# One head pair's gate panels as a unit of seven half-size products

## The chip, the cores and the metric

The kernel runs on one core of a Trainium2 chip. The metric is the device time of one execution in microseconds; the kernel before takes 957.01 us (median of three runs, 956.84 to 957.34).

## What is computed

One sub-layer of a streaming encoder for 512 tokens of width 1024, all in float32:

```python
h = rms_norm(x, norm_g)
proj = h @ w_in            # 1024 x 14,928, split into q, k, v, z, gates of three branches
y_a = mLSTM(...)  * sigmoid(o_a) * silu(z_a)
y_b = dsa_attention(q_b, k_b, v_b, top-k keys of an indexer) * silu(z_b)      # 8 heads of 128
y_m = memory_attention(q_m, k_m, v_m) * silu(z_m)
g   = sigmoid(gate)        # 3 x 1024 columns of proj
out = x + (g[0] * (y_a @ w_branch[0]) + g[1] * (y_b @ w_branch[1]) + g[2] * (y_m @ w_branch[2])) @ w_out
```

The change is in branch B: for each head the kernel needs 128 columns each of q, k, v and z, and beside them it computes 256 of the gate columns.

## The kernel before, in words

Every float32 matrix is used as the sum of a high and a low part (`split`: ScalarE copies the raw tile to a rounded high part, VectorE subtracts that from the raw tile to get the low part). A product is three matmuls per 128 rows of the contraction: high x high, high x low, low x high. The contraction of 1024 is cut into two halves `kh` of KH = 4 blocks. hT_hi and hT_lo hold the normalised input, features on partitions, tokens along the row.

Branch B handles its eight heads in four pairs, i = 0 to 3 (`PAIRS`). For a pair, heads r = 2i and l = 2i + 1:

- **The unit** (`b_unit`, `b_product`, L1185): q, k and v of both heads by seven half-size products instead of eight, after Strassen and Winograd. The raw weights are four blocks a, b, c, d of 4 x 384 columns (a and b: first half of the contraction, c and d: second half). GpSimd makes four sums of them in place (`b_weight_sum`, L3169, four instructions of 384 columns each). Products have tokens as the stationary and weights as the moving operand, 2 x 12 matmuls of 384 columns, into the PSUM banks `main` (0, 1) and `other` (2, 3). Between products ScalarE copies banks out (`b_save`) and VectorE adds banks to saved parts (`b_add`).
- **The two panels** (`f_panel`, L825): z of one head and 256 gate columns, with weights as the stationary and all 512 tokens as the moving operand: 3 blocks x 2 halves x 12 matmuls of 512 columns, for each of the two heads. ScalarE takes the banks out with SiLU (`z_evac`) and sigmoid (`gate_evac`).
- **Attention of the heads**, as hooks between products: `b_turn_qk` (8 transposes, L1138; waits for `b_rotated`), `b_score` (12 matmuls, L1149; waits for the split q and k), `b_turn_p` (10 transposes, L1157; waits for `b_scaled`), `b_values` (12 matmuls, L1167). Head r is done inside its own pair's panels, head l ("tail") inside the next pair's unit.

Each operand, raw, sum or panel, takes one of three slots (`b_op`), is made high on ScalarE (`b_high(n)`, L1760) and low on VectorE (`b_low(n)`, L2584), and TensorE waits for `op_low >= n + 1`. A slot is free when the product three earlier is done (`b_used`). Before the change a pair has 11 operands, `B_OPS`: 7 of the unit and 4 of the panels.

The order on each engine is written out by hand: `b_body(i)` on ScalarE and on VectorE, a list of sums, squares and powers on GpSimd, loads and stores on SyncE. Each engine takes its list strictly in order. On VectorE `b_rotary(a)` is a sum of squares (L2627), four products with the rotary tables (L2636), two joins (L2398, L2399) and the scaling of the keys (L2642, which sets `b_rotated`); it needs GpSimd's squares (L3200) and power (L3205). `b_maxes` (L2598) finds row maxima of the scores, `b_exps` (L1779, ScalarE) the exponentials, `b_scale_p` (L2606, L2609) sets `b_scaled`. The last pair, i = 3, has two small z panels instead of two wide ones, and then the branch panels follow (`branch_panel`), whose left operand y is loaded back from memory (`merged<-ym_kept`) after pair 3's stores: on SyncE the store of y for the head l of pair 2 stands ahead of that load.

Of the kernel before, what the change touches and what calls it, by code (L numbers as in the profile page):

```python
# [14 lines left out]
P = 128  # L15
S = 512
D = 1024
# [30 lines left out]
A_OPHIGH = A_OPLOW = B_OPS * PAIRS - 2  # L48
A_UDONE, A_TDONE, A_USAVED, A_UADDED, A_UREAD = 14 * PAIRS, 4 * PAIRS, 6 * PAIRS, 6 * PAIRS, 2 * PAIRS
# [65 lines left out]
BF = _plan.take(0, 0, (7, 7, 6, 0))  # L115
# [41 lines left out]
def hybrid_block(nc, x, mem, positions, norm_g, mem_norm_g, w_in, conv_w, conv_b, mlstm_gate_b,  # L157
# [3 lines left out]
    with ctx:  # L161
# [132 lines left out]
        raw_e = w_flat[0][:, :, 1536:2048]  # L294
        raw_f = w_hi_f32[:, :].rearrange("p (h n) -> p h n", h=2)[:, :, 1536:2048]
# [148 lines left out]
        def b_op(op, n):  # L444

            width = D if n >= (PAIRS - 1) * B_OPS + 7 else 1536
            return op[B_SLOT[n % 3]][:, 0:width]

        def b_raw_of(n):

            width = D if n >= (PAIRS - 1) * B_OPS + 7 else 1536
            return b_w[B_RAW[n % B_OPS]][:, 0:width]
# [19 lines left out]
        def b_used(n):  # L472

            i, m = n // B_OPS, n % B_OPS
            if m < PRODUCTS:
                return u_done, 2 * PRODUCTS * i + 2 * m + 2
            j, kh = (m - PRODUCTS) // 2, (m - PRODUCTS) % 2
            if kh == 0:
                return f_half, HALF0 + 2 * i + j + 1
            b = 1 if i == PAIRS - 1 else 2  # L480
            return proj_done[b], BF[2][b] + 2 * i + j + 1
# [33 lines left out]
        def _(sp):  # L515
# [102 lines left out]
            def f_gate_stores(i, j):  # L618
                for b in (1, 2):
                    sp.wait_ge(bank_empty[b], BF[2][b] + 2 * i + j + 1)  # L620
                    gate_store(4 + 2 * (2 * i + j) + b - 1, b - 1)
# [17 lines left out]
            for b in range(4):  # L639
                sp.wait_ge(bank_empty[b], BS[2][b] + 1)  # L640
                gate_store(b, b % 2)
            for i in range(PAIRS):
                n = B_OPS * i
# [24 lines left out]
            n = B_OPS * (PAIRS - 1)  # L668
# [7 lines left out]
            sp.wait_ge(f_half, HALF0 + 2 * PAIRS - 1)  # L676
# [135 lines left out]
        def _(pe):  # L812
# [364 lines left out]
            def b_product(i, m, lhs, to, start, before):  # L1177
                n = B_OPS * i + m
# [10 lines left out]
            def b_unit(i):  # L1189
                main, other = (banks[0], banks[1]), (banks[2], banks[3])  # L1190
                tail = 2 * i - 1
                if i:
                    b_turn_qk(tail)
                b_product(i, 0, h_block(0, 0), main, True,
                          lambda t: (bank_empty[t], BF[2][t] + 2 * i) if i else (bank_empty[t], BS[2][t] + 1))
                if i:
                    b_score(tail)
                b_product(i, 1, h_block(KH, 0), other, True,
                          lambda t: ((bank_empty[2], BF[2][2] + 2 * i), (u_added, 6 * i))[t] if i else (bank_empty[2 + t], BS[2][2 + t] + 1))
                if i == 0:  # L1200
                    pe.wait_ge(s_low, 3)
                b_product(i, 2, h_sum(0), main, False, lambda t: (u_saved, 6 * i + t + 1))
                if i:
# [2114 lines left out]
```

## Time and profile before

| | us |
|---|---|
| median of three runs | 957.01 |
| the profiled execution's own time | 957.17 |
| its span (first to last instruction) | 955.4 |
| TensorE busy in it | 950.4 |
| VectorE / ScalarE / GpSimd busy | 735.9 / 544.7 / 351.4 |

Times inside the execution count from the start of the span. A pair takes some 73 us of it; pair 2, the "third pair", has its unit from 375.11 to 409.31 us, its panels to 447.91, and pair 3's unit runs from 448.70 to 482.89. "Busy" of TensorE counts a matmul from its start to its modelled end, and matmuls overlap, so the spacing of starts is what a product costs: a count over the length of a window.

### The profile page before, as it was taken

The numbers are of one execution on the slowest core, as the hardware profiler recorded it, in microseconds if no ns is written. First come the engines' busy times: TensorE is split into PE (matmuls) and PEld (weight loads), VectorE is DVE, ScalarE is ACT, GpSimd is POOL, SyncE is SP. The second block draws the span as 40 slices with busy tenths as digits, with TensorE's granted clock in tenths as the row PEclk, the third lists the DMA queues.
The fourth block names the chain that finished last, engine by engine and source line by source line (L and its number), as shares of the span: only waits on it lengthen the run. The fifth ranks groups of instructions, "written<-read, shape, count | busy, mean of one in ns | idle before, by whom it ended". The sixth has DMA issues, their size and how long they took to land.

```text
span 955.4 us, 13764 instructions
## 1 busy us (share of the span) xinstructions
PE 950.4 (99%) x5041; PEld 843.6 (88%) x5041; DVE 735.9 (77%) x1110; ACT 544.7 (57%) x834; POOL 351.4 (37%) x246
## 2 busy tenths in 40 slices
PE   9999999999999999999999999999999999999998
PEld 7888888888989988988988888898998989999887
DVE  6879987688996686685688566796776867984996
ACT  6877644465456546546563422585775957874341
POOL 0200834456227036146120071372613626201930
PEclk9999999999999999999999999999999999999999
DMA  8624222144532531432355324707033150537512
GB/s 286 244 88 132 87 91 70 62 133 133 165 90 66 166 106 60 144 109 78 101 197 177 131 101 155 241 19 214 1 112 120 33 154 1 177 112 299 206 45 88
DMA packets 105158, 119.31 MB, mean 125 GB/s; under 512 B 4772, under 2 KB 80136, under 8 KB 104332
## 3 DMA queue, kind: packets, MB, share of 16 engines
q1 hardware_dynamic: 105084, 118.53, 38.5%
q8 instruction: 36, 0.59, 0.2%
q14 instruction: 22, 0.18, 0.1%
q10 hardware_dynamic: 16, 0.00, 0.0%
HBM read 106.45 MB, written 12.07 MB: 124 GB/s over the span
## 4 chain that ended last, share of the span: by engine, by line
PE 97%; DVE 1%; DMA 1%; POOL 0%; issue 0%; ACT 0%; SPq 0%; POOLq 0%
PE proj L825 41%; PE proj L1185 11%; PE proj L1319 9%; PE att L1340 7%; PE proj L1340 5%; PE att L1430 3%; PE proj L1378 3%; PE proj L995 2%; PE att L1149 2%; PE att L1167 2%; PE att L1092 1%; PE att L1378 1%; PE att L1114 1%; PE proj L1276 1%; PE att L1157 1%; PE att L1138 1%
## 5 line engine op out<-in xcount | busy, mean ns | idle before, releaser
L825 PE MATMUL proj<-hT_hi,w_hi 128*128 128x512 f32 x264 | 104.0, 394 | 0.0
L825 PE MATMUL proj<-hT_hi,w_lo 128*128 128x512 f32 x264 | 103.1, 390 | 0.0
L825 PE MATMUL proj<-hT_lo,w_hi 128*128 128x512 f32 x264 | 102.9, 390 | 0.0
L2233 DVE TENSOR_TENSOR w_lo<-w_raw,w_hi 128x2048 fp32r<-128x2048 f32 x25 | 62.3, 2492 | 42.2 <-ACT w_hi L1480 40.1
L1480 ACT ACTIVATE w_hi<-w_raw 128x2048 fp32r<-128x2048 f32 x24 | 45.9, 1914 | 55.9 <-PE proj L825 54.4
L825 PE MATMUL proj<-y_hi,w_hi 128*128 128x512 f32 x192 | 75.2, 391 | 0.0
L825 PE MATMUL proj<-y_hi,w_lo 128*128 128x512 f32 x192 | 74.8, 390 | 0.0
L825 PE MATMUL proj<-y_lo,w_hi 128*128 128x512 f32 x192 | 74.7, 389 | 0.0
L825 PEld LDWEIGHTS proj<-hT_hi,w_lo 128*128 128x128 f32 x264 | 49.6, 188 | 10.5
L825 PEld LDWEIGHTS proj<-hT_lo,w_hi 128*128 128x128 f32 x264 | 49.6, 188 | 9.9
L825 PEld LDWEIGHTS proj<-hT_hi,w_hi 128*128 128x128 f32 x264 | 49.6, 188 | 9.8
L3169 POOL TENSOR_TENSOR w_raw<-merged,w_raw 128x384 f32<-128x384 f32 x32 | 36.2, 1164 | 54.6 <-DVE w_lo L2584 31.5
L1967 ACT ACTIVATE w_hi<-w_raw 128x1536 fp32r<-128x1536 f32 (+1 forms) x21 | 29.1, 1385 | 40.6 <-DMA w_raw<-w_in_in 13.0
L2801 DVE TENSOR_TENSOR w_lo<-w_raw,w_hi 128x1536 fp32r<-128x1536 f32 (+1 forms) x21 | 35.1, 1669 | 21.9 <-ACT w_hi L1967 21.9
L3241 POOL TENSOR_TENSOR w_raw<-merged,w_raw 128x384 f32<-128x384 f32 x32 | 40.3, 1302 | 29.5 <-DVE w_lo L2801 29.5
L825 PEld LDWEIGHTS proj<-y_hi,w_lo 128*128 128x128 f32 x192 | 36.0, 188 | 7.6
L825 PEld LDWEIGHTS proj<-y_hi,w_hi 128*128 128x128 f32 x192 | 36.1, 188 | 7.4
L825 PEld LDWEIGHTS proj<-y_lo,w_hi 128*128 128x128 f32 x192 | 36.1, 188 | 7.2
L2813 DVE SCALAR_TENSOR_TENSOR negmask<-proj,small,negmask 128x511 f32<-128x511 f32 (+2 forms) x48 | 35.5, 747 | 4.0 <-ACT negmask L2000 2.8
L1319 PE MATMUL proj<-hT_hi,w_hi 128*128 128x512 f32 x96 | 37.6, 392 | 0.0
L1319 PE MATMUL proj<-hT_hi,w_lo 128*128 128x512 f32 x96 | 37.4, 390 | 0.0
L1319 PE MATMUL proj<-hT_lo,w_hi 128*128 128x512 f32 x96 | 37.4, 390 | 0.0
(591 smaller groups left out, 3145.6 us busy)
## 6 DMA issues: line engine op xcount, KB each, us to landing
w_raw<-w_in_in SPq DMA_DIRECT2D x36, 512.0 KB, 4.6
w_raw<-w_in_in SPq DMA_DIRECT2D x56, 256.0 KB, 3.8
w_raw<-w_branch_in SPq DMA_DIRECT2D x12, 1024.0 KB, 6.6
merged<-w_in_in SPq DMA_DIRECT2D x38, 256.0 KB, 3.7
merged<-w_in_in SPq DMA_DIRECT2D x18, 512.0 KB, 6.3
w_raw<-w_mem_kv_in SPq DMA_DIRECT2D x10, 512.0 KB, 7.1
yF<-x_in SPq DMA_DIRECT2D x8, 512.0 KB, 10.5
w_raw<-w_in_in SPq DMA_DIRECT2D x4, 1024.0 KB, 5.0
```

Of the source, the lines that this page charges most:

```text
L825: ins = mm(ps, lhs[a](k, k0), rhs[b](k, k0), start=(first and k == 0 and j == 0), stop=(last and k == KH - 1 and j == 2))
L1185: ins = mm(to[t][:, 0:UNIT_N], lhs[a](k, t), w[b][:, k, :], start=(start and k == 0 and j == 0), stop=(k == KH - 1 and j == 2), skip_group ...
L1319: ins = mm(banks[b][:, :], w[a][:, k, e * P:(e + 1) * P], hT[b_][:, kh * KH + k, :], start=(kh == 0 and k == 0 and j == 0), stop=(kh == 1 ...
L1340: ins = mm(to[t][:, 0:UNIT_N], lhs[a](k, t), w[b][:, k, :], start=(start and k == 0 and j == 0), stop=(k == KH - 1 and j == 2), skip_group ...
L1378: ins = mm(to[f][:, 0:HALF_T], w[a][:, k, f * P:(f + 1) * P], rhs[b](k), start=(start and k == 0 and j == 0), stop=(k == KH - 1 and j == 2 ...
L1480: A_(w_hi[:, kh, :, 0:n], w_raw[:, kh, :, 0:n], ACT.Copy).then_inc(w_hi_done, 1)
L1967: A_(operand(op_hi, n), raw_of(n, first), ACT.Copy).then_inc(op_high, 1)
L2233: V.tensor_tensor(w_lo[:, kh, :, 0:n], w_raw[:, kh, :, 0:n], w_hi[:, kh, :, 0:n].bitcast(F32), ALU.subtract).then_inc(w_lo_done, 1)
L2801: V.tensor_tensor(operand(op_lo, n), raw_of(n, first), operand(op_hi, n).bitcast(F32), ALU.subtract)\
L2813: ins = V.scalar_tensor_tensor(acc[:, lag:], u[:, 0:S - lag], hcw[:, CONV - 1 - lag, b:b + 1], acc[:, lag:], ALU.mult, ALU.add)
L3169: ins = G.tensor_tensor(b_w[out][:, at], b_w[left][:, at], b_w[right][:, at], op)
L3241: ins = G.tensor_tensor(dst[:, at], left[:, at], right[:, at], ALU.subtract)
```

## The change

For pair 2 alone (`F_UNITS = (2,)`) the two panels are computed together as one more unit of seven products (`f_unit`). The two operands' columns are the two panels (z and 256 gate columns of one head, 384 in all), the two halves of the tokens take the place of the other dimension. The weights are the stationary operand and 256 tokens (or a sum of token blocks that is already there) the moving one: 3 blocks x 12 matmuls of 256 columns a product. The pair then has 14 operands and 8 weight sums. Results are collected in the tiles where z and the gates end up, `f_save` and `f_add`; SiLU and sigmoid are applied to them in SBUF afterwards, in the next pair's body (`f_silu`, `f_sigmoid`). The rotary join of both heads of pair 2 is cut in halves and uses other memory. The loads of the next pair's unit wait for the second unit's products. In pair 3's unit head l's hooks each stand one or more products later than in the other pairs. Other edits only replace constants by counts per pair.

```diff
+F_UNITS = (2,)
+B_N, B_U, B_T = pair_counts(B_OPS, 2 * PRODUCTS), pair_counts(2 * PRODUCTS, 4 * PRODUCTS), pair_counts(4, 8)
# SyncE
+            def f_unit_loads(i):
+                n = B_N[i]
+                for slot, j, kh, lows in (("b", 1, 0, 4), ("a", 0, 0, 5), ("d", 1, 1, 6), ("c", 0, 1, 7)):
+                    sp.wait_ge(op_low, n + lows)
+                    f_load(slot, i, j, kh)
+                y_store(2 * i - 1)
+                for slot, lows in (("b", 4), ("a", 5), ("d", 6), ("c", 7)):
+                    sp.wait_ge(op_low, n + PRODUCTS + lows)
+                    unit_load(slot, i + 1)
+                y_store(2 * i)
...
# TensorE, b_unit; late = i - 1 in F_UNITS
-                if i:
+                if i and not late:
                     b_turn_qk(tail)
...
-                if i:
+                if i and not late:
                     b_score(tail)
                 b_product(i, 1, ...)
+                if late:
+                    b_turn_qk(tail)
                 b_product(i, 2, ...)
-                if i:
+                if late:
+                    b_score(tail)
+                elif i:
                     b_turn_p(tail)
                 b_product(i, 3, ...)
...
                 b_product(i, 4, ...)
+                if late:
+                    b_turn_p(tail)
                 b_product(i, 5, ...)
+                if late:
+                    b_values(tail)
                 b_product(i, 6, ...)
+            def f_product(i, m, rhs, to, start, before, mid=None):
+                n = B_N[i] + PRODUCTS + m
...
+                pe.wait_ge(op_low, n + 1)
+                for part, blocks in enumerate(((0,), (1, 2))):
+                    if part and mid is not None:
+                        mid()
+                    pe.wait_ge(*before(part))
+                    for f in blocks:
+                        at = slice((f - blocks[0]) * HALF_T, (f - blocks[0] + 1) * HALF_T)
+                        for k in range(KH):
+                            for j, (a, b) in enumerate(((0, 0), (0, 1), (1, 0))):
+                                ins = mm(to[part][:, at], w[a][:, k, f * P:(f + 1) * P], rhs[b](k), ...)
+                    ins.then_inc(u_done, 1)
+            def f_unit(i):
+                f_product(i, 0, f_half_block(0, 0), main, True, lambda t: (u_read, B_R[i] + t + 1))
+                f_product(i, 1, f_half_block(KH, 0), other, True, lambda t: (u_added, B_S[i] + t + 5))
+                f_product(i, 2, f_half_sum(0), main, False, lambda t: (u_saved, done + t + 1), lambda: b_turn_qk(r))
+                b_score(r)
+                f_product(i, 3, f_half_sum(1), main, False, lambda t: (u_saved, done + t + 3))
+                f_product(i, 4, f_half_sum(2), other, True, lambda t: (u_added, done + t + 1))
+                b_turn_p(r)
+                f_product(i, 5, f_half_sum(3), other, False, lambda t: (u_saved, done + t + 5))
+                b_values(r)
+                f_product(i, 6, f_half_block(KH, HALF_T), main, False, lambda t: (u_added, done + t + 3))
# ScalarE, b_body of the pair after
+                if i - 1 in F_UNITS:
+                    f_silu(i - 1)
+                    b_high(n + 2)
+                    act.wait_ge(b_vlow, 2 * i)
+                    b_save(i, 0, main, b_raw[:, 0:2])
+                    b_high(n + 3)
+                    b_qk_high(tail)
+                    f_sigmoid(i - 1)
+                    b_save(i, 2, main, b_second)
+                    b_high(n + 4)
+                    b_high(n + 5)
+                    b_exps(tail)
+                    b_high(n + 6)
+                    b_save(i, 4, other, b_fifth)
                     b_probs_high(tail)
# ScalarE, second unit of pair 2, after b_last_copy(i)
+                    f_save(i, 0, 0, ...); f_save(i, 0, 1, ...)
+                    b_high(n + 9)
+                    b_high(n + 10)
+                    f_save(i, 2, 0, ...); b_qk_high(r); f_save(i, 2, 1, ...)
+                    b_high(n + 11)
+                    b_exps(r)
+                    b_high(n + 12)
+                    f_save(i, 4, 0, ...); b_high(n + 13); f_save(i, 4, 1, ...)
+                    b_probs_high(r)
+                    b_high(n + 14)
+                    b_high(n + 15)
+                    b_values_high(l)
+                    f_save(i, 6, 0, ...); f_save(i, 6, 1, ...)
# VectorE, b_body of the pair after
+                if i - 1 in F_UNITS:
+                    b_turned_parts(tail)
+                    b_values_low(tail)
+                    b_low(n + 2)
+                    b_key_scale(tail)
+                    b_finish(tail - 1)
+                    b_low(n + 3)
                     b_qk_low(tail)
+                    b_add(i, 1, (banks[2], banks[3]), b_raw[:, 0:2], 1)
+                    b_low(n + 4)
                     b_maxes(tail)
+                    b_low(n + 5)
+                    b_low(n + 6)
                     b_scale_p(tail)
                     b_probs(tail)
+                    b_add(i, 3, ...); b_low(n + 7); b_add(i, 5, ...); b_low(n + 8)
                     b_finish(tail)
# VectorE, second unit of pair 2, after b_low(n + 8)
+                    b_norm_sum(r)
+                    b_turned_parts(r)
+                    b_low(n + 9)
+                    b_key_scale(r)
+                    b_low(n + 10)
+                    b_values_low(r)
+                    b_qk_low(r)
+                    f_add(i, 1, other, 0, 0, 1)
+                    b_maxes(r)
+                    b_low(n + 11)
+                    b_norm_sum(l)
+                    b_scale_p(r)
+                    b_low(n + 12)
+                    b_low(n + 13)
+                    f_add(i, 3, main, 1, 1, 5)
+                    b_probs(r)
+                    b_low(n + 14)
+                    f_add(i, 5, other, 1, 0, 3)
+                    b_low(n + 15)
# GpSimd, pair 2
                 b_late_sum(i)
+                if i in F_UNITS:
+                    b_first_sums(i, 1)
+                    b_squares(2 * i)
+                    b_second_sum(i, 1)
+                    b_power(2 * i)
+                    b_third_sum(i, 1)
+                    b_late_sum(i, 1)
+                    b_squares(2 * i + 1)
+                    b_power(2 * i + 1)
+                    b_early_sums(i + 1)
+                    continue
```

## Rows read from the trace of the kernel before

**Rows 1.** The page, busy time by engine: us, share of the span, instructions.

```profile
PE 950.4 (99%) x5041; PEld 843.6 (88%) x5041; DVE 735.9 (77%) x1110; ACT 544.7 (57%) x834; POOL 351.4 (37%) x246
```

**Rows 2.** Waits of TensorE, whole span: us in total, times, longest.

```profile
PE att L978 <- POOL ident L3107: 1.5, 1, 1.5
```

**Rows 3.** Busy by window: window, length, TensorE busy (instructions), clock, DMA share, GB/s.

```profile
409.31:447.91 38.60, 38.60 (x187) 1.00 0.31 87
448.70:482.89 34.19, 34.19 (x205) 1.00 0.31 101
```

**Rows 4.** Busy by window, line 825 alone (512 columns), in the panels of pair 2.

```profile
409.31:417.51 8.20, 8.20 (x36) 1.00 0.44 120
```

**Rows 5.** Busy by window, line 1378 alone (256 columns), weights stationary.

```profile
834.81:846.32 11.51, 11.51 (x96) 1.00 0.39 125
```

**Rows 6.** Chain of waits in the panels, one hook: start, us, line.

```profile
424.02 1.91 PE att L1149 x12
```

**Rows 7.** The page's costliest groups: one weight load, mean ns after the busy time.

```profile
L825 PEld LDWEIGHTS proj<-hT_hi,w_lo 128*128 128x128 f32 x264 | 49.6, 188 | 10.5
```

**Rows 8.** Timeline of GpSimd, pair 2: start, us, line, operation.

```profile
406.05 1.04 POOL L3200 TENSOR_TENSOR arena<-yF 128x512 f32<-128x512 f32 x1 [21.10 <-DVE yF L2591]
...
421.58 2.02 POOL L3205 TENSOR_TENSOR small<-small,minus_half 128x8 f32<-128x8 f32 x1 [1.54 <-DVE small L2628]
436.57 3.94 POOL L3169 TENSOR_TENSOR w_raw<-merged,w_raw 128x384 f32<-128x384 f32 x4 [12.96 <-DVE w_lo L2584]
```

**Rows 9.** Timeline of VectorE, panels of pair 2.

```profile
409.64 1.22 DVE L2627 TENSOR_REDUCE small<-arena 128x8 f32<-128x1024 f32 x1 [0.93 <-POOL arena L3200]
...
410.97 0.69 DVE L2636 TENSOR_TENSOR arena<-yF,tabs 128x512 f32<-128x512 f32 x1
...
415.72 0.43 DVE L2656 TENSOR_TENSOR b_vl<-yF,b_vh 128x256 fp32r<-128x256 f32 x1
...
426.16 0.29 DVE L2598 CUSTOM_DVE_ANT_0 score<-att,negmask 128x128 f32<-128x128 f32 x1
...
428.01 1.75 DVE L2584 TENSOR_TENSOR w_lo<-merged,w_hi 128x1536 fp32r<-128x1536 f32 x1
...
433.54 1.27 DVE L2609 TENSOR_SCALAR score<-score,small 128x128 f32<-128x128 f32 x4
```

**Rows 10.** Timelines of VectorE and GpSimd where both work, pairs 0 and 2.

```profile
259.75 2.43 DVE L2584 TENSOR_TENSOR w_lo<-w_raw,w_hi 128x1536 fp32r<-128x1536 f32 x1 [0.30 <-ACT w_hi L1760]
...
259.52 1.04 POOL L3200 TENSOR_TENSOR arena<-yF 128x512 f32<-128x512 f32 x1 [16.16 <-DVE yF L2591]
260.52 2.56 POOL L3200 TENSOR_TENSOR arena<-merged 128x512 f32<-128x512 f32 x1
...
446.14 2.31 DVE L2656 TENSOR_TENSOR b_vl<-arena,b_vh 128x256 fp32r<-128x256 f32 x2
...
446.00 3.32 POOL L3169 TENSOR_TENSOR merged<-merged,w_raw 128x384 f32<-128x384 f32 x3
```

**Rows 11.** Timeline of ScalarE, pair 2 and the start of pair 3.

```profile
430.63 0.49 ACT L1779 ACTIVATE score<-score,small 128x128 f32<-128x128 f32 x1
...
433.11 0.19 ACT L1779 ACTIVATION_READ_ACCUMULATOR score<-score,small 128x1 f32 x1
...
446.12 1.28 ACT L1825 ACT_TABLE_LOAD   x1
...
449.58 1.49 ACT L1760 ACTIVATE w_hi<-w_raw 128x1536 fp32r<-128x1536 f32 x1
```

**Rows 12.** DMA issues, 470 to 500 us: count, KB each, us to landing.

```profile
merged<-ym_kept SPq DMA_DIRECT2D x1, 1536.0 KB, 7.1
```

**Rows 13.** Timeline of VectorE, first low part of the first branch panel.

```profile
491.19 2.29 DVE L2233 TENSOR_TENSOR w_lo<-w_raw,w_hi 128x2048 fp32r<-128x2048 f32 x1
```

**Rows 14.** Busy by window at the start: TensorE's first transposes.

```profile
1.54:4.77 3.23, 3.23 (x15) 1.00 0.76 228
4.77:5.60 0.83, 0.83 (x7) 1.00 0.92 311
```

More of the change, by code:

```diff
@@ L47, with pair_counts @@
 B_LOADS = 80
-A_OPHIGH = A_OPLOW = B_OPS * PAIRS - 2
-A_UDONE, A_TDONE, A_USAVED, A_UADDED, A_UREAD = 14 * PAIRS, 4 * PAIRS, 6 * PAIRS, 6 * PAIRS, 2 * PAIRS
+F_UNITS = (2,)
+def pair_counts(panels, unit):
+    return [sum(unit if j in F_UNITS else panels for j in range(i)) for i in range(PAIRS + 1)]
+B_N, B_U, B_T = pair_counts(B_OPS, 2 * PRODUCTS), pair_counts(2 * PRODUCTS, 4 * PRODUCTS), pair_counts(4, 8)
+B_S, B_R, B_F = pair_counts(6, 12), pair_counts(2, 10), pair_counts(2, 0)
+A_OPHIGH = A_OPLOW = B_N[PAIRS] - 2
+A_UDONE, A_TDONE, A_USAVED, A_UADDED, A_UREAD = B_U[PAIRS], B_T[PAIRS], B_S[PAIRS], B_S[PAIRS], B_R[PAIRS]
 A_SMADE, A_SHIGH, A_SLOW = 1, 4, 4
@@ L1792, in b_probs_high @@
                 ph = b_pT[0][:, :].rearrange("p (b n) -> p b n", n=P)
-                if a % 2 == 0:
+                if a % 2 == 0 and a // 2 not in F_UNITS:
                     act.wait_ge(b_rotated, a + 2)
@@ L1833, in start_gates, with f_save @@
                     A_(sig[:, b % 2], banks[b][:, :], ACT.Sigmoid).then_inc(bank_empty[b], 1)
+            def f_save(i, m, part, src, j, half):
+                th = slice(half * HALF_T, (half + 1) * HALF_T)
+                act.wait_ge(u_done, B_U[i] + 2 * PRODUCTS + 2 * m + part + 1)
+                if part == 0:
+                    act.wait_ge(yb_sent[j], SENT0 + 16 * i)
+                    return A_(f_z(i, j)[:, th], src[0][:, 0:HALF_T], ACT.Copy)
+                for b in range(2):
+                    act.wait_ge(gate_sent[b], SENT0 + 16 * (2 + 2 * i))
+                return A_(f_gates(j)[:, :, th], src[1][:, :].rearrange("p (b n) -> p b n", b=2), ACT.Copy)
@@ L1835, in b_body, with f_silu, f_sigmoid @@
+            def f_silu(i):
+                act.wait_ge(u_added, B_S[i] + 12)
+                act.wait_ge(u_read, B_R[i] + 4)
+                for j in range(2):
+                    A_(f_z(i, j), f_z(i, j), ACT.Silu).then_inc(u_read, 1)
+            def f_sigmoid(i):
+                for j in range(2):
+                    for b in range(2):
+                        A_(f_gates(j)[:, b], f_gates(j)[:, b], ACT.Sigmoid).then_inc(u_read, 1)
             def b_body(i):
-                n, last = B_OPS * i, i == PAIRS - 1
+                n, last = B_N[i], i == PAIRS - 1
@@ L2644, in b_rotary, with f_add @@
                 then(V.tensor_scalar(b_ns[a % 2], r2[:, :, 0], -(B_HD ** -0.5), None, ALU.mult))
+            def b_rotary(a):
+                b_norm_sum(a)
+                b_turned_parts(a)
+                b_key_scale(a)
+            def f_add(i, m, src, j, half, saved):
+                th = slice(half * HALF_T, (half + 1) * HALF_T)
+                parts = ((f_z(i, j)[:, th], src[0][:, 0:HALF_T]),
+                         (f_gates(j)[:, :, th], src[1][:, :].rearrange("p (b n) -> p b n", b=2)))
+                for part, (dst, bank) in enumerate(parts):
+                    dve.wait_ge(u_saved, B_S[i] + 6 + saved + part)
+                    dve.wait_ge(u_done, B_U[i] + 2 * PRODUCTS + 2 * m + part + 1)
+                    V.tensor_tensor(dst, bank, dst, ALU.add).then_inc(u_added, 1)
             def b_qk_low(a):
@@ L3185, in b_late_sum, with b_first_sums @@
-            def b_late_sum(i):
-                pool.wait_ge(t_done, 4 * i + 3)
-                pool.wait_ge(op_low, B_OPS * i + 3)
+            def b_first_sums(i, second):
+                n, loads = B_N[i] + PRODUCTS * second, B_LOADS * i + 48 + 32 * second
+                if i and not second:
+                    pool.wait_ge(op_low, n + 1)
+                pool.wait_ge(raw_landed["b"], loads)
+                pool.wait_ge(raw_landed["d"], loads)
+                b_weight_sum("b", "d", "b", ALU.subtract)
```

292 lines of the change are left out of this document (191 added, 101 removed).

## The prediction, as it was written before the kernel ran

> **What bounds the kernel now.** I read the share of each engine first: TensorE is busy 99% of the span, VectorE 77%, ScalarE 57%, GpSimd 37% [rows 1]. Then TensorE's waits: they come to under 3 us in all, the longest 1.5 us at the start, and the others are of 0.3 and less [rows 2]. So whatever TensorE is spared is gained, and whatever it is made to wait is lost; no slack in it swallows either. Then busy time by window for pair 2's panels and pair 3's unit, both without a gap [rows 3]. The rest of the prediction asks two questions: how much shorter is TensorE's list, and do ScalarE, VectorE and GpSimd, with more to do in less time and in another order, still deliver each operand before it is wanted. Clock times below are those of the trace before; F is the end of the new unit's seventh product.
>
> **Removed and added on TensorE.** Gone: 2 x 72 = 144 matmuls of 512 columns, which start every 8.20 / 36 = 0.228 us [rows 4]: 32.8 us. Added: 7 x 36 = 252 matmuls of 256 columns. Line 1378 runs just these (weights stationary, 256 tokens moving) and starts one every 11.51 / 96 = 0.120 us [rows 5]: 30.2 us. Gain 2.6 us, not an eighth of 32.8 (4.1), because 0.120 is more than half of 0.228. The hooks are the same four, 5.6 us in all, the scores 1.9 of it [rows 6]. The Trainium skill (TensorE: Matmul & The Clock Gate, "Wait — 56ns, not 53.3ns?") puts the spacing at columns / 2.4 GHz plus 2.5 ns, 0.216 and 0.109 us, by which the gain would be an estimated 3.6 us. The two rows are 0.011 to 0.012 longer at both widths, so each short matmul pays the floor in full; I take the rows.
>
> **What VectorE and GpSimd do to each other.** GpSimd gets four more weight sums, 3.94 us each when alone, 0.97 an instruction [rows 8], and VectorE three more low parts of 1.75 [rows 9]. These are not simply side by side. A low part that begins while a GpSimd instruction runs takes 2.43 instead of 1.75, and GpSimd's next takes 2.56 instead of 1.04; two value low parts of 0.43 take 2.31 together while three sum instructions take 3.32 instead of 2.9 [rows 9, 10]. So instructions of VectorE that read two SBUF operands and GpSimd's take turns, one of each; I charge VectorE 0.85 a turn (2.56 less the 1.7 of the low part). Low parts, rotary products, joins, key scale and value low parts pay it; those that read PSUM don't.
>
> **Stall 1, third product of the new unit.** It wants `b_low(n + 9)`, which now stands behind `b_turned_parts(r)`. The squares began at 406.05 and the sum of squares at 409.64 [rows 8, 9]. The new first weight sum runs in front of them and delays a low part by 0.7, so the squares end at 410.4 and the table products begin 1.3 later, 411.7. Alone they and the four half joins take 4 x 0.61 + 4 x 0.35 + 0.2 = 4.1 [rows 9]. Sum 2 and the start of sum 3 fall beside them and beside the low part: four to five turns, 3.7. Low part 1.65. End: 421.1. TensorE gets there at 409.31 + 72 x 0.12 = 417.95. Stall 3.1. With no turns the low part ends at 417.5: 0. With one more turn: 4.
>
> **Stall 2, scores of r.** After that low part come key scale (0.85 with its two small ones), a low part 1.65, values 0.7, and the low parts of q and k 1.3: 4.5, and four turns, since sums 3 and 4 run back to back: 7.9. TensorE needs 36 x 0.12 + 0.8 of transposes + 0.1 = 5.2. Stall 2.6; 0 without turns, 3.4 with one more.
>
> From there to F each operand arrives in time by 0.5 to 3 us: the weight sum 4, ScalarE's copies of 0.4 to 0.6, and the fused exponentials (no table change between) come first.
>
> **Stall 3, transposes of l in pair 3's unit.** `b_turn_qk(l)` now wants the key scale, behind the parts, values and a low part of that unit. The last operand of the new unit's list can be made high only after its sixth product, F - 6.2 (values 1.9 and a product 4.3 remain), and is low at F - 2.3. From there VectorE has 2.4 + 1.4 + 0.7 + 1.65 + 0.6 = 6.8 of its own. Sums 1 to 3 of the next unit, which before were over by then, could not start until F - 5.9: twelve instructions, ten still to come, ten turns: 8.5. Key scale at F + 13.0. TensorE is there after two products, (34.19 - 4.8 of hooks, three of the four) / 7 = 4.2 each [rows 3]: F + 8.4. Stall 4.6. Without turns F + 7, or F + 9 if sum 2 ends late: 0 to 0.6; with the key scale waiting too, 5.5.
>
> **Stall 4, transposes of p in pair 3's unit.** This one is made by order alone. From the end E of the transposes: q and k high 0.9; SiLU was done, but `f_sigmoid` stands next: table 1.28 and four of 0.5 to 0.6, 3.4; the second copy of `b_save(i, 2)` waits for the third product, E + 4.55, and ends at 4.95; `b_high(n + 4)` 6.4; its low part 8.1; maxima and bias 1.9, 10.05 (426.16 to 428.01); exponentials 2.6, 12.7 (430.63 to 433.2); `b_high(n + 6)` 14.15; its low part 15.9; reciprocal and first scaling 16.4, last 17.35 [rows 9, 11]. TensorE is there at E + 3 x 4.2 + 1.9 = 14.5, and the last four transposes end at 17.8 instead of 15.6. Stall 2.2, bounds 1.5 and 3.
>
> **Stall 5, first branch panel.** The low part of its weights ended at 493.48 [rows 13] and was wanted at 482.89 + 48 x 0.228 + 0.8 = 494.6: 1.1 to spare. On SyncE the store of l's y stands ahead of `merged<-ym_kept` (7.1 us) [rows 12], and `b_finish(l)` has moved behind `b_low(n + 8)`, to 2.4 before pair 3's unit ends, where the load had been issued 9.8 before. It lands 5 to 8 after that end, beside the branch weights; ScalarE's copies of it stand in front of the weights' high part: low part 11.7 to 14.3 after, wanted at 11.8. Stall 1.3, bounds 0 and 2.5.
>
> **The sum.** 3.1 + 2.6 + 4.6 + 2.2 + 1.3 = 13.8 us of stalls, less 2.6: +11.2. On the profiled execution's 957.17 that is 968.4, and the median is 0.16 lower: 968.2. The two extra table loads and the SBUF activations lie on ScalarE, 57% busy, and cost nothing but where stall 4 counts them.
>
> **Rivals.** (a) The turns cost little, because GpSimd gets through between VectorE's instructions: stalls 1 to 3 shrink to 0.3, 0 and 0.3, those by order stay: +1.4, some 958.5. The short `power` beside three table products cost VectorE nothing [rows 8, 9], which speaks for it; the shared pieces in [rows 10] against. Half of the turns give 963. (b) Faster: every wait fits, only TensorE's list counts: 954.4. It decides at one place, `b_scale_p(l)`: the chain from the transposes of l to it must be under 14.5 and not 16.4. For it: before, no operand was ever late [rows 2], and ScalarE could be ahead if the weights' copies came early. Against: its lists are strict, and durations in the chain vary by under 0.1. (c) The clock. The granted clock of all rows is 1.00, the 2.4 GHz level, but the first 15 matmuls took 3.23 us and the next 7 only 0.83 [rows 14], 0.215 against 0.119. If a gap of 3 to 5 us brings the slow pace back for a similar 3.2 us, each costs 1.6; for stalls 1 and 3, 971.4. No gap of that length lies within the work before, so the trace can't say. The same page of the Trainium skill ("Why this matters for your kernels") warns that idle gaps between bursts of matmuls take the clock back to half. (d) The change doesn't do what it says: if 256 columns went at the 0.188 of a weight load [rows 7], 252 would cost 47.4, +17, and 985 with the stalls. The rate of line 1378 shows the opposite [rows 5].
>
> **How the numbers follow.** Forecast 0.55 (its own range 963 to 973), (a) 0.25, (b) 0.10, (c) 0.08, (d) 0.02. The range of 8 in 10 goes from 958 to 973: it takes in (a), the bounds of the stalls and (c), and leaves out (b) and (d). A measurement of this kernel tells 0.2%, 1.9 us, from no change. Faster by more: 0.09, from (b). Within: 0.05, the low end of (a). Slower: 0.86.
>
> **What would show it.** TensorE's waits would name `b_low` (L2584's successor) before the third product of pair 2's second unit, the low parts of q and k before r's scores, the key scale before l's transposes, and the scaling of p before l's last transposes, 2 to 5 us each. Line `f_product` would start every 0.120 us. Sum instructions of GpSimd and table products of VectorE would take 1.2 to 1.5 us side by side in place of 0.97 and 0.69. It is wrong if the window of the 252 matmuls with its hooks is 36 us long and l's transposes begin at once; and the clock rival holds if matmuls behind a gap start at twice their spacing.

## The result, and the profile after

The changed kernel takes 969.98 us (median of 4 runs, 968.80 to 971.05), the kernel before, timed beside it, 956.92 (956.65 to 957.34). The ratio is 1.0136 [1.0118, 1.0153]: 13.1 us slower, inside the range of 958 to 973 and 1.8 above the 968.2 of the forecast. The profiled execution took 969.57 us with a span of 967.7, against 957.17 and 955.4.

First the page's busy times, which answer to [rows 1]: TensorE has 2 us more although its list is shorter, VectorE 19 more and GpSimd 18.5 more.

```profile
PE 952.5 (98%) x5149; PEld 851.2 (88%) x5149; DVE 754.7 (78%) x1123; ACT 548.2 (57%) x842; POOL 369.9 (38%) x262
```

Then TensorE's waits (line and what was waited for: us in total, times, longest). In [rows 2] the wait for `ident` was the longest; four longer ones stand ahead of it now, and they are the forecast's stalls 3, 1, 4 and 2.

```profile
PE att L1181 <- DVE arena L2824: 4.2, 1, 4.2
PE proj L1295 <- DVE b_op_lo L2746: 2.8, 1, 2.8
PE att L1200 <- DVE score L2771: 1.6, 1, 1.6
PE att L1192 <- DVE b_kl L2846: 1.6, 1, 1.6
PE att L1021 <- POOL ident L3346: 1.5, 1, 1.5
PE proj L1228 <- ACT yF L1869: 0.5, 1, 0.5
```

Busy time by window (window, length, TensorE and its weight loads busy, clock, DMA share, GB/s), first of line 1295 (`f_product`) alone: 72 matmuls of 256 columns in 8.64 us, 0.120 each, as in [rows 5].

```profile
431.75:440.39 8.64, 8.64 (x72) 8.59 (x71) 1.00 0.37 96
```

The same view over the stretch where three of the four stalls lie (columns: window, its length, busy time of TensorE, its weight loads, VectorE, ScalarE and GpSimd with instructions, granted clock, DMA share, GB/s), before and after. VectorE is busy 55.3 of 60 us with 67 instructions, where 75 instructions had taken 42.8: 0.83 an instruction and not 0.57. They are not the same instructions; e9 below, which has those of this kernel, gives 0.62 (52.0 us for 84).

```profile
405.00:465.00 60.00, 60.00 (x319) 53.64 (x318) 42.79 (x75) 36.82 (x55) 30.11 (x22) 1.00 0.31 87
```

```profile
405.00:465.00 60.00, 51.47 (x373) 50.51 (x372) 55.29 (x67) 28.75 (x43) 42.24 (x31) 0.97 0.20 53
```

VectorE's timeline after shows which instructions have grown (start, us, engine, line, operation). Of the four table products the second and third take 0.8 more than the one in [rows 9], and the last of the four half joins 0.8 more than the three before it; the low part that TensorE waits for takes 2.43, and the key scale behind it, 0.7 elsewhere, 1.49.

```profile
412.24 0.68 DVE L2811 TENSOR_TENSOR arena<-yF,tabs 128x512 f32<-128x512 f32 x1
412.84 1.50 DVE L2811 TENSOR_TENSOR arena<-merged,tabs 128x512 f32<-128x512 f32 x1
414.27 1.50 DVE L2811 TENSOR_TENSOR w_lo_f<-yF,tabs 128x512 f32<-128x512 f32 x1
...
417.08 0.42 DVE L2560 TENSOR_TENSOR arena<-arena,w_lo_f 128x256 f32<-128x256 f32 x1
417.42 1.25 DVE L2561 TENSOR_TENSOR arena<-arena,w_lo_f 128x256 f32<-128x256 f32 x1
418.70 2.43 DVE L2746 TENSOR_TENSOR b_op_lo<-w_raw,b_op_hi 128x1536 fp32r<-128x1536 f32 x1
421.05 1.49 DVE L2824 TENSOR_TENSOR arena<-arena,small 128x512 f32<-128x512 f32 x1
...
451.22 2.93 DVE L2811 TENSOR_TENSOR arena<-arena,tabs 128x512 f32<-128x512 f32 x2
454.07 2.92 DVE L2811 TENSOR_TENSOR w_lo_f<-arena,tabs 128x512 f32<-128x512 f32 x2
...
458.08 1.23 DVE L2561 TENSOR_TENSOR arena<-arena,w_lo_f 128x256 f32<-128x256 f32 x1
```

In the full timeline VectorE is never idle for 0.1 us from 410.38 to 429.6, where the low parts of q and k end, nor from 448.65 to 464.67, where the key scale of l ends: in front of stalls 1 to 3 it waits for no late sum, its own instructions take longer.

GpSimd's timeline, same kernel. A weight sum of four instructions takes 3.94 alone [rows 8] and 4.8 to 6.7 where VectorE's products, joins and low parts stand beside it: each side pays.

```profile
410.31 4.90 POOL L3408 TENSOR_TENSOR w_raw<-w_raw 128x384 f32<-128x384 f32 x4
...
417.24 6.17 POOL L3408 TENSOR_TENSOR merged<-merged,w_raw 128x384 f32<-128x384 f32 x4
...
449.76 6.68 POOL L3408 TENSOR_TENSOR w_raw<-w_raw 128x384 f32<-128x384 f32 x4
456.52 4.80 POOL L3408 TENSOR_TENSOR merged<-merged,w_raw 128x384 f32<-128x384 f32 x4
```

And windows laid on the granted clock's record. It stood at 0.50, the 1.2 GHz level, for 3.4 us behind the first stall and for 3.4 behind the third. TensorE was busy in all of both, so each costs 1.7 us of work.

```profile
421.50:424.90 3.40, 3.40 (x18) 3.40 (x17) 3.37 (x4) 0.42 (x2) 3.32 (x4) 0.50 0.00 0
465.80:469.20 3.40, 3.40 (x13) 3.40 (x12) 3.40 (x4) 3.37 (x6) 3.40 (x3) 0.50 0.20 77
```

**Where 12.3 us of span come from.** The distance between the starts of two neighbouring matmuls, less their usual spacing, gives the four stalls as 2.9, 1.7, 4.4 and 1.8 us (stalls 1 to 4); a fifth, small one of 0.7 stands in pair 0's unit (the wait for `yF`), and at the first branch panel 0.1 is left. With 3.4 for the clock (twice half of 3.4): 955.4 - 2.7 (the list, measured below) + 10.8 + 0.7 + 0.1 + 3.4 = 967.7.

### The profile page after: what moved, and what is told of

It is laid out like the page before. It is cut to its first block, busy times and chain, and to the rows that moved or that the text cites. A ratio compares the mean times of both kernels' runs of the same rounds, so it can differ in the third digit from the quotient of the medians.

```text
span 967.7 us, 14035 instructions
## 1 busy us (share of the span) xinstructions
PE 952.5 (98%) x5149; PEld 851.2 (88%) x5149; DVE 754.7 (78%) x1123; ACT 548.2 (57%) x842; POOL 369.9 (38%) x262
## 4 chain that ended last, share of the span: by engine, by line
PE 89%; DVE 5%; issue 2%; DMA 1%; ACT 1%; POOL 1%; SPq 0%; DVEq 0%; ACTq 0%; POOLq 0%
PE proj L868 37%; PE proj L1421 9%; PE proj L1228 8%; PE att L1442 7%; PE proj L1442 5%; PE att L1532 3%; PE proj L1480 3%; PE proj L1038 2%; PE att L1192 1%; PE att L1135 1%; PE att L1480 1%; PE att L1157 1%; DVE w_lo L2746 1%; PE att L1210 1%; PE proj L1378 1%
## 5 line engine op out<-in xcount | busy, mean ns | idle before, releaser
L868 PE MATMUL proj<-hT_hi,w_hi 128*128 128x512 f32 x228 | 89.7, 394 | 0.0
L868 PE MATMUL proj<-hT_hi,w_lo 128*128 128x512 f32 x228 | 89.0, 390 | 0.0
L868 PE MATMUL proj<-hT_lo,w_hi 128*128 128x512 f32 x228 | 88.8, 390 | 0.0
L3408 POOL TENSOR_TENSOR w_raw<-merged,w_raw 128x384 f32<-128x384 f32 x40 | 46.1, 1185 | 65.3 <-DVE w_lo L2746 27.0
L3504 POOL TENSOR_TENSOR w_raw<-merged,w_raw 128x384 f32<-128x384 f32 x32 | 40.3, 1299 | 29.6 <-DVE w_lo L3040 29.6
L868 PEld LDWEIGHTS proj<-hT_hi,w_lo 128*128 128x128 f32 x228 | 42.8, 188 | 9.1
L868 PEld LDWEIGHTS proj<-hT_lo,w_hi 128*128 128x128 f32 x228 | 42.9, 188 | 8.5
L868 PEld LDWEIGHTS proj<-hT_hi,w_hi 128*128 128x128 f32 x228 | 42.8, 188 | 8.5
L1421 PE MATMUL proj<-hT_hi,w_hi 128*128 128x512 f32 x96 | 37.6, 392 | 0.0
L1421 PE MATMUL proj<-hT_hi,w_lo 128*128 128x512 f32 x96 | 37.5, 390 | 0.0
L1421 PE MATMUL proj<-hT_lo,w_hi 128*128 128x512 f32 x96 | 37.4, 390 | 0.0
```

Of the source, the lines that this page charges most:

```text
L868: ins = mm(ps, lhs[a](k, k0), rhs[b](k, k0), start=(first and k == 0 and j == 0), stop=(last and k == KH - 1 and j == 2))
L1421: ins = mm(banks[b][:, :], w[a][:, k, e * P:(e + 1) * P], hT[b_][:, kh * KH + k, :], start=(kh == 0 and k == 0 and j == 0), stop=(kh == 1 ...
L3408: ins = G.tensor_tensor(b_w[out][:, at], b_w[left][:, at], b_w[right][:, at], op)
L3504: ins = G.tensor_tensor(dst[:, at], left[:, at], right[:, at], ALU.subtract)
```

## The experiments

My theory: the unit of seven is in itself 2.6 us shorter, and is made slower by two things only, the turns that VectorE's instructions with two SBUF operands and GpSimd's take (stalls 1 to 3), and one place of fixed order (stall 4), with the clock's fall behind the gaps on top. The rivals: the turns are not it, and VectorE has simply too much to do; the gain is not there; the clock costs nothing of its own.

**e1: light weight sums.** Three quarters of the work of every weight sum from pair 2's second unit on are left out.

```
             def b_weight_sum(...):
-                for k in range(KH):
+                for k in range(1 if light[0] else KH):
```

> The changed kernel, but from the first sum for the new unit of pair 2 on, GpSimd computes only the first of the four column blocks of each weight sum (so those products get unsummed weights); all waits and the order stay. If taking turns between GpSimd and VectorE makes stalls 1 to 3, they go from 3.0, 1.8 and 4.4 us to under 0.5 each, stall 4 stays at 1.9, with no long gap the granted clock stays at full, and the time is 957 to 958. If the lists' order or late operands make them, stalls 1 and 3 keep more than half their length and the time stays above 963.

Measured: 956.80 us (956.50 to 958.88, 10 runs), ratio 1.0003 [0.9994, 1.0013]; profiled span 954.7. Stalls 1, 2 and 3 are gone together, and stall 4 alone is left:

```profile
PE att L1200 <- DVE score L2771: 1.9, 1, 1.9
```

VectorE has the same instructions to do as after; in its timeline the table products are back at 0.7 and the low part at 1.76, and it ends at 417.2 instead of 421.1:

```profile
411.79 0.68 DVE L2811 TENSOR_TENSOR w_lo_f<-yF,tabs 128x512 f32<-128x512 f32 x1
...
415.49 1.76 DVE L2746 TENSOR_TENSOR b_op_lo<-w_raw,b_op_hi 128x1536 fp32r<-128x1536 f32 x1 [0.26 <-ACT b_op_hi L1863]
```

So it is GpSimd's instructions beside them, not VectorE's own list, that make the operands late. The Trainium skill (GPSIMD Engine Reference, "1. Specifications") says that GpSimd shares its SBUF interfaces with VectorE and contends with those of its instructions that have two SBUF inputs; the traces agree, with 1.50 against 0.69.

**e2: scale first.** In pair 3's unit VectorE takes the maxima of p ahead of one low part and its scaling ahead of another.

```
-                    b_low(n + 4)
                     b_maxes(tail)
+                    b_low(n + 4)
                     b_low(n + 5)
-                    b_low(n + 6)
                     b_scale_p(tail)
+                    b_low(n + 6)
```

> The changed kernel with another order on VectorE in pair 3's unit: the row maxima of l ahead of the low part of the fifth operand, the scaling of p ahead of the low part of the seventh. If stall 4 is VectorE's order (its low parts in front of maxima and scaling), it goes from 1.9 us to under 0.2 and the time falls by 1.7 to 2 (968.1, less what the clock adds or spares by chance). If it is ScalarE's list (sigmoid and copies ahead of the exponentials), at least 1.2 of it stays.

Measured: 967.76 us (966.75 to 968.30), ratio 1.0109 [1.0092, 1.0126]. TensorE's waits no longer hold line 1200; the others stay as they were:

```profile
PE att L1181 <- DVE arena L2824: 3.9, 1, 3.9
PE proj L1295 <- DVE b_op_lo L2746: 2.9, 1, 2.9
PE att L1192 <- DVE b_kl L2846: 1.5, 1, 1.5
```

Stall 4 is made by the order of VectorE's list, and is worth its 2 us.

**e9: both.** Light sums (left out as in e1) and scaling first.

> The changed kernel with both edits together: GpSimd computes only the first of the four blocks of every weight sum from pair 2's second unit on (the other three are left out of the computation), and in pair 3's unit VectorE scales the probabilities of pair 2's first head ahead of the low part of the seventh operand. With light sums alone one stall was left, 1.9 us in front of the last transposes of pair 3's unit (span 954.7); scaling first took that stall away by itself. My theory: the stalls are of two kinds, turns taken with GpSimd's sums and one place of fixed order, and nothing else is lost; then no gap over 0.5 us is left in TensorE's list but the start's, the span is 955.4 - 2.6 = 952.8 us, the time 954.5 and the clock 1.00 throughout. That is also what the shorter list is worth when every operand comes in time. Rival: VectorE is so full that what is taken from one wait comes back at another; then the time stays at 956 to 957. A second rival: the 2.6 us of the shorter list are not there in full; then the span without gaps is over 953.5.

Measured: 954.31 us (954.02 to 954.74, 8 runs), ratio 0.9973 [0.9963, 0.9984]; span 952.7, clock 1.00 throughout. No wait over 0.6 us is left but the one at the start, and over the stretch in which the changed kernel stood for 8.5 us TensorE is busy all the time:

```profile
405.00:465.00 60.00, 60.00 (x438) 59.56 (x437) 52.04 (x84) 38.98 (x60) 17.44 (x13) 1.00 0.29 85
```

This is the faster kernel that the change would be if the sums cost nothing: 955.4 - 952.7 = 2.7 us, the 2.6 that the two spacings gave. The sums are part of the computation, so it is no version to use. It also shows that VectorE could do its 84 instructions of the stretch in 52 of 60 us.

**e3: the gaps filled.** TensorE runs 24 matmuls of 256 columns, read by nobody, in stall 1 and 36 in stall 3.

```
+            def keep_busy(a, times):
+                pe.wait_ge(b_pcopied, a * 4)
+                for _ in range(times):
+                    mm(att[0][:, 0:HALF_T], hT[0][:, 0, 0:P], hT[0][:, 0, 0:HALF_T], start=True, stop=True)
```

> The changed kernel with matmuls nobody reads in the two long gaps of TensorE: 24 of 256 columns (2.9 us) ahead of the new unit's third product and 36 (4.3 us) ahead of l's transposes. If the two stretches at half clock follow from those gaps, the clock stays at full, twice 1.7 us come back, and the time is 966.5, steadier from run to run. If the clock falls for another reason, the time stays at 970 and two stretches remain.

Measured: 971.16 us (970.93 to 971.35), ratio 1.0145 [1.0128, 1.0162]. My 966.5 was a miss. The clock did stay up where the gaps were filled, but it fell behind the two others, by windows:

```profile
429.50:432.90 3.40, 3.38 (x12) 3.21 (x13) 2.10 (x8) 1.05 (x1) 1.53 (x2) 0.50 0.15 43
484.10:487.50 3.40, 3.40 (x14) 3.40 (x14) 2.44 (x6) 2.47 (x5) 0.00 (x0) 0.51 0.00 0
```

TensorE's waits say why the first of these two gaps grew: with the clock up it has done the third product 1.8 us earlier (426.1 against 427.9), and VectorE delivers only 0.2 earlier.

```profile
PE att L1192 <- DVE b_kl L2853: 3.1, 1, 3.1
PE att L1200 <- DVE score L2778: 1.9, 1, 1.9
```

Two things follow. In the changed kernel the first fall costs nothing, since stall 2 swallows its 1.7 us. And falls came here behind gaps of 3.39 and 2.28 us (start to start), so keeping the clock would take filling these too, and filling gives back none of the time of a gap.

**e4: finer sums.** Every weight sum in 8 instructions of 192 columns instead of 4 of 384.

```
-                for k in range(KH):
-                    at = slice(k * UNIT_N, (k + 1) * UNIT_N)
+                for k in range(2 * KH):
+                    at = slice(k * UNIT_N // 2, (k + 1) * UNIT_N // 2)
```

> The changed kernel with every weight sum cut into eight GpSimd instructions of 192 columns instead of four of 384. If each VectorE instruction waits for one GpSimd instruction, its wait falls from some 0.85 us to 0.45: stalls 1 to 3 shrink from 9.2 us together to 3 to 5, and with shorter gaps one or both half-clock stretches go: 961 to 965. If it is the total of GpSimd's work that delays (each sum must be through before VectorE goes on), nothing changes or it gets 1 us slower for eight starts: 970 to 971.

Measured: 975.03 us (974.79 to 976.15), ratio 1.0189 [1.0172, 1.0206], slower where I had expected 961 to 965. Timelines of GpSimd (three sums, of eight instructions each) and of VectorE:

```profile
413.93 6.55 POOL L3408 TENSOR_TENSOR w_raw<-w_raw 128x192 f32<-128x192 f32 x8
422.23 8.29 POOL L3408 TENSOR_TENSOR merged<-merged,w_raw 128x192 f32<-128x192 f32 x8
430.60 4.52 POOL L3408 TENSOR_TENSOR w_raw<-merged,w_raw 128x192 f32<-128x192 f32 x8
```

```profile
416.18 1.08 DVE L2811 TENSOR_TENSOR arena<-merged,tabs 128x512 f32<-128x512 f32 x1
```

The half that I had in mind is there: a turn costs VectorE 0.4 instead of 0.8, since the instruction that it waits for is shorter, and the waits of stalls 1 to 3 shrink to 1.5, 0.9 and 3.0. The half that I had not counted is GpSimd's. Where VectorE only reads PSUM (430.60), a sum takes 4.52, 0.56 an instruction, little more than the 3.94 of four. But a sum now has twice as many places at which a VectorE instruction gets in front: the two beside VectorE's products, joins and low parts take 6.55 and 8.29, where the changed kernel has 4.90 and 6.17. So now the sums themselves are late: 2.9 us in pair 0's unit, 2.0 at the new unit's fourth product, and stall 4 grows to 2.7.

```profile
PE att L1181 <- DVE arena L2824: 3.0, 1, 3.0
PE proj L1228 <- ACT yF L1869: 2.9, 1, 2.9
PE att L1200 <- DVE score L2771: 2.7, 1, 2.7
PE proj L1295 <- DVE w_lo L2746: 2.0, 1, 2.0
```

The other part of the loss is the clock: its record has four falls of 3.4 us and not two, at 248.9, 440.1, 467.4 and 487.9, one of them behind the gap of 2.30 us (start to start) at the fourth product. The gaps are 14.0 us in all against 11.5, and two more falls are 3.4: together they are the 5.4 us by which this span is longer, within 0.5. The window of the second fall:

```profile
440.10:443.45 3.35, 3.35 (x18) 3.35 (x17) 3.31 (x7) 2.23 (x3) 1.64 (x1) 0.50 0.80 227
```

**e5: the third sum later.** The order of e2, and on GpSimd the next unit's third sum waits until the keys of head l are scaled (`b_rotated`), so that it no longer runs beside l's rotary products and joins; its first sum starts earlier.

```
-                if i and not second:
+                if i and not second and i - 1 not in F_UNITS:
                     pool.wait_ge(op_low, n + 1)
...
                 b_second_sum(i, 0)
+                if i - 1 in F_UNITS:
+                    pool.wait_ge(b_rotated, 2 * i)
                 b_third_sum(i, 0)
```

> The changed kernel with VectorE's order of the run before (maxima and scaling of l first) and two moves on GpSimd: the first weight sum for pair 3 starts when its blocks have landed, not after pair 3's first low part, and the third waits until l's keys are scaled. By the theory of turns VectorE's rotary products of l then meet four sum instructions at most instead of ten: stall 3 goes from 4.4 to under 0.5, stall 4 to under 0.2, stalls 1 and 2 stay at 3.0 and 1.6 to 1.9, one half-clock stretch is left: 961 to 962. If stall 3 comes from the length of VectorE's own list, it keeps 2 us or more and the time is above 963.5.

Measured: 964.93 us (963.94 to 965.23), ratio 1.0078 [1.0062, 1.0095], some 3 us above the 961 to 962 that I had expected. Stall 3 goes from 4.2 to 0.7, as the turns say, but part of it comes back two products later:

```profile
PE proj L1295 <- DVE b_op_lo L2746: 2.8, 1, 2.8
PE att L1192 <- DVE b_kl L2846: 1.6, 1, 1.6
...
PE proj L1228 <- DVE b_op_lo L2746: 1.5, 1, 1.5
PE att L1181 <- DVE arena L2824: 0.7, 1, 0.7
```

The last sum was now finished at 471.32 (GpSimd's timeline), and its high and low part stand behind it:

```profile
467.39 3.93 POOL L3408 TENSOR_TENSOR w_raw<-merged,w_raw 128x384 f32<-128x384 f32 x4
```

**e7: head r's work later.** e5, and in pair 2's second unit the rotary parts of r, its scores, transposes and values moved one or two products later on all engines, and GpSimd's second sum ahead of r's squares, so that the low parts come first.

> The run e5_late_unit plus a new order in pair 2's second unit: GpSimd makes the second sum ahead of r's squares and the power after the fourth sum; VectorE makes the low parts of the third and fourth operands ahead of r's rotary products and the joins after the fifth; TensorE does r's four hooks one to two products later. By the theory of turns (each operand gets ahead of the shared stretch) stalls 1 and 2 shrink from 4.8 to 1 to 2 us together, no gap is long enough to lower the clock, and the time is 955 to 958. If VectorE and GpSimd together are simply full in this stretch, the stalls come back elsewhere, at r's scaling or the seventh product, and the time stays at 960 or more.

Measured: 963.77 us (962.58 to 964.77), ratio 1.0073 [1.0056, 1.0089], not 955 to 958. The profiled execution, 962.58, is the fastest of the four and has no fall of the clock; two of the others, 964.33 and 964.77, have a mean granted clock of 0.996. The stalls have other names and 6.4 us in all:

```profile
PE att L1181 <- DVE arena L2827: 2.5, 2, 2.1
PE proj L1295 <- DVE w_lo L2746: 2.4, 1, 2.4
...
PE proj L1228 <- DVE b_op_lo L2746: 1.5, 1, 1.5
```

With four more sums put beside VectorE's table products and low parts, one or the other is late wherever they stand. Three orders were tried (e2, e5, e7) and none brought the pair back to the time of before; that no order can is not shown.

**e8: sigmoid early.** The prediction's chain for stall 4 has `f_sigmoid`, 3.4 us, ahead of `b_save`, though by its numbers the third product ends later. Here it stands right behind `f_silu`.

```
                     f_silu(i - 1)
+                    f_sigmoid(i - 1)
...
-                    f_sigmoid(i - 1)
```

> The changed kernel with ScalarE's sigmoids of the gates moved from between l's q and k copies and the bank copies to right behind the SiLUs, 12 us earlier. By the prediction's chain of stall 4 this gives nothing, because the bank copy behind them waits for the third product until E + 4.55 anyway: stall 4 stays at 1.6 to 2 and the time at 970. If ScalarE's list is the cause of stall 4, it falls by 1.5 us or more.

Measured: 969.54 us (968.80 to 970.69), ratio 1.0131 [1.0114, 1.0148], and line 1200 waits 1.6 us as after. The sigmoid is no part of stall 4: ScalarE waits for the third product anyway.

This run shows one thing more. Its clock stood at half for 6.8 us from 420.5 on, with TensorE at work in 5.9 of them, where the changed kernel has 3.4, and the span is 967.7 all the same: stall 2 has shrunk from 1.6 to 0.5, about as much as TensorE lost.

```profile
PE att L1192 <- DVE b_kl L2846: 0.5, 1, 0.5
```

**e6 and e10: a gap in the kernel before.** TensorE waits ahead of pair 2's second product for the four exponentials of the tail head (e6) or for the first one only (e10). Nothing else is changed, so the clock is measured without the new unit.

```
+                if i == 2:
+                    pe.wait_ge(b_exp, 4 * tail + 4)      # e10: 4 * tail + 1
```

> The kernel before, with one wait added: TensorE begins the second product of pair 2's unit only when l's exponentials of pair 1 are done (385.4 instead of 381.3), a gap of 4.1 us with all operands there. If a gap of this length takes the clock to its 1.2 GHz level, one stretch of 3.4 us at half follows and the time is 957.0 + 4.1 + 1.7 = 962.8; if a gap costs only itself, 961.1, and the granted clock stays at 1.00.

> The kernel before (not the changed one) with a single wait added on TensorE: ahead of the second product of pair 2's unit it waits for the first of the four exponentials of the tail head, not for all four as in the earlier run of this kind, whose gap was 4.2 us and after which the granted clock stood at 0.5 for 6.8 us. From that run's trace the first exponential ends near 382.7 us, where the product begins at 380.8 when not held: a gap of 2.0 us. If the clock falls only after gaps longer than that, the time is 957.0 + 2.0 = 959.0 and the clock record shows no fall. If a gap of 2 us is enough at whatever place, a stretch of 3.4 us at 0.5 follows, 1.7 us more: 960.7. In the changed kernel a gap of 1.9 to 2.3 us was followed by a fall in one kernel and not in others, so I give the fall 4 in 10.

Measured: e6 963.49 us (963.16 to 964.24), ratio 1.0068 [1.0051, 1.0085]; e10 960.68 (958.02 to 961.00, 9 runs), 1.0029 [1.0020, 1.0039]. The waits of TensorE and the windows of the half clock, e6:

```profile
PE proj L1185 <- ACT score L1781: 4.0, 1, 4.0
```

```profile
383.00:389.80 6.80, 5.02 (x16) 5.02 (x17) 0.94 (x2) 1.73 (x6) 1.24 (x1) 0.50 0.38 116
```

and e10:

```profile
PE proj L1185 <- ACT score L1781: 1.9, 1, 1.9
```

```profile
384.00:387.40 3.40, 3.40 (x13) 3.40 (x12) 0.56 (x1) 1.08 (x4) 0.61 (x1) 0.50 0.73 226
```

The stall of 4.0 us costs 6.3, its own length and 2.3 for the slow pace behind it. That of 1.9 costs 3.7 to 4.0 in five of the nine runs (960.7 to 961.0), 1.9 + 1.7 and a little more, and 1.0 to 2.4 in the other four; the mean granted clock is 0.998 in the five and 1.00 in the four. So the same wait is followed by a fall in some executions and not in others. The trace is of one of the five (gap of 2.34 us, start to start); how long the gap was in the four isn't on record, and it may have been shorter. e1, with one gap of 2.28 us, has the two kinds too: six runs at 956.5 to 956.8 with a clock of 1.00, among them the profiled one, whose record has no fall, and four at 958.3 to 958.9 with 0.998. As e3 has a fall behind a gap of the same 2.28 us, the length of a gap alone does not decide.

## Why the prediction was right

| term | forecast | measured (after) | shown by |
| --- | --- | --- | --- |
| TensorE's list | -2.6 | -2.7 | span of e9 |
| stall 1, third product | 3.1 | 2.9 | gone in e1 |
| stall 2, scores of r | 2.6 | 1.7, or 3.3 with the clock up | gone in e1; e3 |
| stall 3, transposes of l | 4.6 | 4.4 | gone in e1, 0.7 in e5 |
| stall 4, transposes of p | 2.2 | 1.8 | stays in e1, gone in e2 |
| stall 5, branch panel | 1.3 | 0.1 | trace |
| pair 0's unit | 0 | 0.7 | trace |
| clock | 0 (rival c) | 3.4 | clock record, e6, e10 |
| sum | 11.2 | 12.3 | |

**The gain** was right: the spacing at half the width is more than half, and the row of line 1378 held for the new line within 0.001. The estimate of 3.6 us by the spacing of the Trainium skill (TensorE: Matmul & The Clock Gate, "Wait — 56ns, not 53.3ns?") is 0.9 us too large.

**The turns** (stalls 1 to 3) were right in place and owner and near in size. `b_low(n + 9)` was forecast to end at 421.1 and ended at 421.13; the key scale of l was forecast 13.0 us behind F (452.02 in this trace) and came 12.7 behind. Within the second figure two errors cancel, which is luck. The low part in front of l's products ended at F - 0.7 and not at F - 2.3: ScalarE had waited for the load of its block (3.26 us idle, until `merged<-w_in_in` had landed), which the prediction had at nothing. And behind it the turns took 6.6 us and not 8.5, eight and not ten: 13.4 us in all, 6.8 of them VectorE's own work. e1 makes all three stalls vanish at once, and there the key scale comes 7.1 behind F, the forecast's F + 7 without turns. Rival (a) is out, with one part of it true: the short `power` costs VectorE nothing.

**Stall 4** was right in place and near in size, and the chain held as its numbers have it: e8 takes the sigmoid out of it and nothing moves; the links that count are the third product, its copy, the low part, and VectorE's order behind it, as e2 shows.

**Stall 5** was mis-sized. The load of `ym_kept` was issued 2.4 us ahead of the unit's end, as forecast, but it landed 4.8 behind that end (7.1 less the 2.4 give 4.7), ahead of the 5 to 8 that I had allowed; the weights' low part ended 11.8 behind it (506.98), just when it was wanted (506.94). VectorE's timeline of after, its row answering to [rows 13]:

```profile
504.69 2.29 DVE L2395 TENSOR_TENSOR w_lo<-w_raw,w_hi 128x2048 fp32r<-128x2048 f32 x1 [1.48 <-ACT w_hi L1582]
```

I had put the stall in the middle of 0 and 2.5; it was at the low bound.

**Stall 2** was under-sized: with the clock up it is 3.3 (e3), not 2.6, the forecast's own bound with one more turn. In the changed kernel only 1.7 of it are left, because TensorE, slow behind stall 1, gets there later.

**The clock** was given 0.08 as rival (c), as something beside the forecast. It happened with the stalls and not instead of them: falls of 3.4 us at half clock, 1.7 each, behind stalls 1 and 3, as (c) had them by place and price (971.4 in all). By its numbers the kernel as profiled, 969.57, lies between the forecast and (c), because stall 5 was missing and stall 2 swallowed the first fall. That it was under a tenth was the weakest judgement of the prediction: the rows at the start [rows 14] showed the two paces, and the Trainium skill (TensorE: Matmul & The Clock Gate, "Why this matters for your kernels") warns that idle gaps between bursts bring the clock back to half. The runs agree: falls came behind gaps of 2.28 us (e3) to 4.55 us (stall 3), though not behind every one.

**How much of the match is luck.** The mechanism of the four stalls and the gain is shown. That the median came within 1.8 us is in part luck: 3.4 us of clock and 0.7 in pair 0's unit, which the sum had at nothing, stand against 1.2 too much for stall 5, 0.9 for stall 2 (which the clock shortened) and 0.9 for the other three stalls and the list together. Without the slow stretches stall 2 would have been 3.3 and the span some 1.8 us shorter, an estimate from the table.

**Rival (b)**, every wait fits, is what e9 measured, 954.31 against its 954.4. In the changed kernel it failed where it was said to be decided, at `b_scale_p(l)`, and at three places before that.

## What to carry to other kernels

Trading TensorE's columns for sums on GpSimd pays only if the sums fall where VectorE has no instruction with two SBUF operands to do: for each pair that meets, count 0.8 us on VectorE, and on GpSimd some 0.5 beside a table product (4.90 for a sum of 3.94 with two such meetings) to 1.5 beside a low part (2.56 for 1.04 [rows 10]), before believing that the engine has room (VectorE was at 77%). Cutting GpSimd's instructions finer lowers VectorE's price and raises GpSimd's (e4). Halving a product's width gives back less than half its time, here 0.120 of 0.228, which left 2.7 us to win against 15.8 of new sums on GpSimd (4 x 3.94) and 6.6 more on VectorE (742.5 busy in e9, 735.9 before). And a stall on a TensorE that was never idle can cost more than its length: for each gap of the lengths seen here, 2.3 us and more, charge 1.7 us on top (2.3 in e6, behind a gap of 4.4), unless another stall follows close behind and swallows it.

## What was not expected of the hardware

- The granted clock fell behind gaps as short as 2.28 us (e3, start to start), in e10 and e1 in some executions of the same kernel and not in all; in e7 gaps of 2.72, 2.47 and 1.86 us had none in the profiled execution. Every fall in the stretches looked at lasted 3.4 or 6.8 us.
- Filling a gap did not save its fall: e3 kept the clock up through two gaps, and it fell behind the two others instead, at the same 3.4 us each.
- GpSimd's cost by width: 0.56 us for 192 columns (4.52 / 8, e4) and 0.98 for 384 (3.94 / 4 [rows 8]), so half the width is 0.57 of the time, not far from TensorE's 0.53. What makes the finer sums dear is what they take beside VectorE, 6.55 and 8.29 against 4.90 and 6.17.
